# Moving the position transform of a hybrid encoder layer into the tiles of the projection's second half, and cutting the copies of the bias rows into 24

## The chip, the cores and the metric

The kernel runs on one core of one Trainium2 chip. The metric is the device time of one execution in microseconds (us). A profiled execution gives a trace of every instruction on the engines: PE is TensorE's matmul, PEld its weight load, DVE is VectorE, ACT is ScalarE, POOL is GpSimd, SP is SyncE, whose queue ("SPq") issues all the data transfers of this kernel.

## The reference

One layer of an encoder over two sequences of 4096 and 2048 tokens ("a" and "b"), with a model width of 1024:

```python
h = rmsnorm(x, norm_g)
proj = h @ w_in
q, k, v, g_attn, u, g_four = jnp.split(proj, [768, 1536, 2304, 3072, 3328], axis=-1)
# attention: 12 heads, three dilated windows, merged by their denominators; gated by silu(g_attn)
uf = u.astype(jnp.float32).reshape(B, S, N_FOURIER_GROUPS, FOURIER_GROUP)
mixed = jnp.fft.fftn(uf, axes=(1, 3), norm="ortho").real
four = jnp.einsum('bsgc,gce->bsge', mixed.astype(x.dtype), w_four).reshape(B, S, D_FOURIER)
four = four * jax.nn.silu(g_four)
y = jnp.concatenate([attn, four], axis=-1) @ w_out
return x + y
```

The change concerns the transform over positions (axis 1 of `fftn`) and the table of attention biases.

## The kernel before

`build` runs six stages one after the other; each is a block of five engine programs, and the engines meet between blocks: `setup`, `project(core, 0)`, `project(core, 1)`, `fourier`, `attention`, `combine`.

**The projection's first half** goes through 48 tiles of 128 tokens. Per tile it loads x (`load_x`, two tiles ahead), normalizes, splits into a high and a low part (`p_h_hi`, `p_h_lo`), keeps both parts in scratch memory for the second half (`keep_h`), and multiplies by the columns of q, k and u: four products per tile in the order 3, 0, 1, 2, each of 8 x 3 matmuls (`product`, L474). Product 3 is u (256 columns); it is transformed over channels at once (`turn_u` L481, `channel_dft` L489) and stored as `scratch_ab`, 512 floats per token. Behind the last weight load and ahead of `load_x(2)`, SP issues three transfers (L368) which write each row of 384 biases 128 times into `scratch_line`: 12 heads x 128 copies x 1536 bytes, for three dilations.

On DVE, tile 0 is special: the copy that `channel_dft(0)` waits for (L743) stands behind `norm_x(2)` and `head_norm(0, c=2)`. On ACT `norm_x(2)` (L535) stands ahead of the squares of product 2.

**The second half** goes through the same 48 tiles with the columns of v, the gates: per tile `load_h(t + 2)` (two transfers, L340, waiting until the last product of tile t is done), then a wait for the tile's four results, then `store_v` (14 transfers, L389 and L394) and one store of the gate (L433). Tiles 2, 4, 6 and 8 also turn the bias rows (`turn_lines`: a load of 1.5 MB, a copy on POOL, a store of 1.5 MB). The tile loop of PE, ACT and DVE is a hardware loop over two tiles (`Fori`); SP's is written out.

**The stage `fourier`** transforms `scratch_ab` over positions in two levels. A level-1 piece is a slice of columns of all rows, multiplied by one table (128x128 for a, 64x64 for b), and goes to `scratch_g_a` or `scratch_g_b`; a level-2 piece reads that, multiplies each 256 columns by another 128x64 table, and goes to `scratch_four`, which only `combine` reads. Level 2 needs all of level 1 of its sequence. There are 14 pieces of 4096 columns: 4 + 4 of level 1, 4 + 2 of level 2. Six buffers for input, four for output, eight PSUM banks; DVE and ACT copy the banks out in turn (L912). Piece 0 is already loaded during the second half of the projection.

**`attention`** starts with loads (L1104 first) that don't read what `fourier` wrote.

Of the kernel before, what the change touches and what calls it, by code (L numbers as in the profile page):

```python
# [25 lines left out]
P = 128  # L26
D = 1024
HD = 64
NH = 12
# [17 lines left out]
LINE = 384  # L47
VW = HD + 1
# [5 lines left out]
PIECE = 8 * BANK  # L54
# [53 lines left out]
def build(nc, io):  # L108
    core = Core(nc, io)
    with core.keep:  # L110
# [16 lines left out]
        with ExitStack() as spectrum:  # L127
            core.four_in = core.sb(spectrum, "four_in0", [P, PIECE])
            core.four_first = {n: core.sb(spectrum, "four_first_" + n, [2 * seq // N2, 2 * seq // N2])
                               for n, seq in zip("ab", SEQS)}  # L130
            core.four_in_loaded, core.four_table_in = core.sem("four_loaded0"), core.sem("four_table_in")
            project(core, 1)
            fourier(core)
# [81 lines left out]

def project(core, half):
# [22 lines left out]
    else:  # L239
        h_in, ones_done = [S("h_in0"), S("h_in1")], S("ones_done")  # L240
        expo_done, v_tail_done = S("expo_done"), S("v_tail_done")
        line_in, lines_turned, lines_kept = S("line_in"), S("lines_turned"), S("lines_kept")
    stored = [S("stored0"), S("stored1")]
# [21 lines left out]
    def tiles(engine, step):  # L265

        step(0, 0)
        step(1, 1)
        with engine.Fori(1, TILES // 2 - 1) as it:
            step(it * 2, 0)  # L270
            step(it * 2 + 1, 1)
        step(TILES - 2, 0)
        step(TILES - 1, 1)

    with ExitStack() as st:
# [22 lines left out]
        else:  # L298
            rows = [sb(f"v{i}", [P, VROW]) for i in range(2)]
            gate = [sb(f"gate{i}", [P, D]) for i in range(2)]  # L300
            expo, denom = sb("expo", [P, BANK]), sb("denom", [P, BANK])
        ps = [core.ps(st, name(f"ps{c}")) for c in range(4)]
        if half == 0:
            ps_t = [core.ps(st, name(f"ps_t{c}")) for c in range(banks_t)]
            ps_qk = [core.ps(st, name(f"ps_qk{c}")) for c in range(2)]
        block = st.enter_context(nc.Block())
# [17 lines left out]
        def _(sp):  # L324
# [37 lines left out]
            if half == 1:  # L362
                for n in "ab":
                    sp.dma_start(core.four_first[n][:], io["c_first_" + n]).then_inc(core.four_table_in, 16)
# [47 lines left out]
            def step(t, s):  # L412
# [8 lines left out]
                if half == 0:  # L421
# [5 lines left out]
                    if s == 1:  # L427
                        store_qk(t + 1, 0)
                else:
# [3 lines left out]
                    sp.dma_start(dram["gate"][lane_rows(t), :], gate[s][:]).then_inc(stored[s], 16)  # L433

            for t in range(TILES):
                step(t, t % 2)
            if half == 0:
                store_qk(TILES, 1)
                store_qk(TILES, 2)
                for c in range(3):  # L440
                    sp.wait_ge(qk_stored[c], 16 * (TILES // 2))
            else:
                sp.wait_ge(lines_kept, 32)
            if half == 0:
# [4 lines left out]
            if half == 0:  # L449
                sp.wait_ge(lines_out, 16 * len(DILS))  # L450

        @block.tensor
        def _(pe):
# [11 lines left out]
            def product(t, s, c):  # L465
# [10 lines left out]
                ins.then_inc(mm_done[c], 1)  # L476

# [26 lines left out]
            def step(t, s):  # L504
# [27 lines left out]
        def _(act):  # L532
# [49 lines left out]

            def gate_exp(t, c):
# [7 lines left out]
            def step(t, s):  # L591
# [12 lines left out]
                else:  # L604
                    for c in order:
# [3 lines left out]
                        if c > 0:  # L609
                            gate_exp(t, c)  # L610

# [162 lines left out]

class Piece:


    def __init__(self, name, seq, base, level, i):
        self.name, self.seq, self.base, self.level, self.i = name, seq, base, level, i
        self.n1 = seq // N2
        self.rows = 2 * self.n1 if level == 1 else 2 * N2
        self.out_rows = 2 * self.n1 if level == 1 else N2


def fourier_pieces():

    both, each = list(zip("ab", SEQS, BASES)), PIECE // DF  # L790
    return ([Piece(*seq, 1, i) for seq in both for i in range(N2 // each)]
            + [Piece(*seq, 2, i) for seq in both for i in range(seq[1] // N2 // each)])


def load_piece(core, sp, at, to, loaded):

    each = slice(at.i * PIECE // DF, (at.i + 1) * PIECE // DF)
    if at.level == 1:
        src = core.dram["ab"][at.base:at.base + at.seq, :].rearrange("(a b) (s c) -> s a b c", b=N2, s=2)
    else:  # L800
        src = core.dram["g_" + at.name].rearrange("(s k) (n c) -> s n k c", s=2, c=DF)
    half = at.rows // 2
    for part in range(2):
        sp.dma_start(to[part * half:(part + 1) * half, :].rearrange("p (n c) -> p n c", c=DF),
                     src[part, :, each, :]).then_inc(loaded, 16)


def fourier(core):

    nc, io, dram = core.nc, core.io, core.dram
    S = lambda n: core.sem("four_" + n)
    BANKS, IN, OUT = 8, 6, 4
    k1s = PIECE // DF
    pieces = fourier_pieces()
    fine_in = S("fine_in")  # L820
    loaded = [core.four_in_loaded] + [S(f"loaded{i}") for i in range(1, IN)]
    mm_done, out_done = S("mm_done"), [S("dve_out"), S("act_out")]
    stored = [S(f"stored{i}") for i in range(OUT)]
    with ExitStack() as st:
        sb = lambda n, shape: core.sb(st, "four_" + n, shape)
        first = core.four_first
        second = {n: sb("second_" + n, [2 * N2, seq]) for n, seq in zip("ab", SEQS)}
        source = [core.four_in] + [sb(f"in{i}", [P, PIECE]) for i in range(1, IN)]
        result = [sb(f"out{i}", [P, PIECE]) for i in range(OUT)]
        ps = [core.ps(st, f"four_ps{i}") for i in range(BANKS)]  # L830
        block = st.enter_context(nc.Block())

        @block.sync
        def _(sp):
            def load(m):
                if m >= IN:
                    sp.wait_ge(mm_done, BANKS * (m - IN + 1))
                load_piece(core, sp, pieces[m], source[m % IN], loaded[m % IN])

            def store(m):  # L840
                at = pieces[m]
                for evac in out_done:
                    sp.wait_ge(evac, BANKS // 2 * (m + 1))
                have = result[m % OUT][0:at.out_rows, :]
                if at.level == 1:
                    to = dram["g_" + at.name][:, at.i * PIECE:(at.i + 1) * PIECE]
                else:
                    to = dram["four"][at.base:at.base + at.seq, :].rearrange("(b a) c -> b a c", a=at.n1)
                    to = to[:, at.i * k1s:(at.i + 1) * k1s, :]
                    have = have.rearrange("p (k c) -> p k c", c=DF)  # L850
                sp.dma_start(to, have).then_inc(stored[m % OUT], 16)

            def spectrum_stored(name):

                for m, at in enumerate(pieces):
                    if at.level == 1 and at.name == name:
                        sp.wait_ge(stored[m % OUT], 16 * (m // OUT + 1))

            for m in range(1, IN):
                load(m)  # L860
                if m == 4:
                    for n in "ab":
                        sp.dma_start(second[n][:], io["c_second_" + n]).then_inc(fine_in, 16)
            ready = IN
            for m, at in enumerate(pieces):
                store(m)

                while ready < len(pieces) and ready - IN <= m:
                    new = pieces[ready]
                    if new.level == 2:  # L870
                        last_g = max(i for i, x in enumerate(pieces) if x.level == 1 and x.name == new.name)
                        if m < last_g + (1 if new.name == "a" else 0):
                            break
                        if new.i == 0:
                            spectrum_stored(new.name)
                    load(ready)
                    ready += 1
            for i in range(OUT):
                sp.wait_ge(stored[i], 16 * len(range(i, len(pieces), OUT)))

        @block.tensor
        def _(pe):
            pe.wait_ge(core.four_table_in, 32)
            for m, at in enumerate(pieces):
                have = source[m % IN][0:at.rows, :]
                pe.wait_ge(loaded[m % IN], 32 * (m // IN + 1))
                if at.level == 2:
                    pe.wait_ge(fine_in, 32)
                for j in range(BANKS):
# [754 lines left out]
```

## Time and profile before

| | us |
|---|---|
| median of 3 runs | 4076.96 (4073.61 to 4079.73) |
| the profiled execution, its own time | 4074.14 |
| its span in the trace | 4072.4 |
| PE busy in it | 3766.3 (92%) |
| DVE, ACT, POOL busy | 2554.1, 1680.9, 400.9 |

The span is the time from the first to the last record; 1.7 us lie around it. The 40 slices on the page are 102 us each, digits are tenths. In the rows of busy time by stretch the columns are: the stretch and its length, then busy time and (in brackets) instructions of PE, PEld, DVE, ACT and POOL, the clock granted to PE (1.00 is 2.4 GHz, 0.50 is 1.2 GHz), the mean busy share of the DMA engines, and GB/s. A matmul's recorded end is modelled, so the pace of matmuls is better read from the distance of their starts than from their durations.

### The profile page before, as it was taken

To read this page: it belongs to the slowest core of one execution; us is meant where nothing else is said; L and a number is where in the kernel's file an instruction comes from. 1 tells how busy PE (TensorE), PEld (TensorE's weight loads), DVE (VectorE), ACT (ScalarE), POOL (GpSimd) and SP (SyncE) were. 2 spreads that over 40 slices of the span, in tenths; PEclk is the share of its full clock that TensorE was granted. 3 is DMA by queue.
4 is the path that set the end of the run, shared out by engine and by line. 5 is a ranking of instruction groups with operands and counts; after the bars stand their busy time and mean duration, and the time that the engine had idled before them with its cause. 6 is when DMAs were issued, how large, how long until landed. Compare 5 with 4: busy or idle time off the path is not lost. (4 is left out here: it accounts for less than half of the span.)

```text
span 4072.4 us, 100342 instructions
## 1 busy us (share of the span) xinstructions
PE 3766.3 (92%) x38254; PEld 3227.5 (79%) x38254; DVE 2554.1 (63%) x7710; ACT 1680.9 (41%) x4443; POOL 400.9 (10%) x674
## 2 busy tenths in 40 slices
PE   3599999999997999999997859999999999799999
PEld 2488888888886888888884349999989898688887
DVE  3356666666655454445443248888888888777775
ACT  2233333333322111111111148898888888333332
POOL 0000000000000000000000024333342432000000
PEclk7799999999998999999998689999999999899999
DMA  6534444444437554444446996777768675666664
GB/s 131 126 134 154 163 145 140 139 170 142 152 124 234 184 156 141 146 145 144 142 145 168 269 281 169 211 188 188 205 167 214 155 204 137 228 243 244 239 249 175
DMA packets 604151, 721.86 MB, mean 177 GB/s; under 512 B 37215, under 2 KB 473567, under 8 KB 602112
## 3 DMA queue, kind: packets, MB, share of 16 engines
q1 hardware_dynamic: 603840, 717.55, 59.1%
q8 instruction: 215, 3.52, 0.4%
q14 instruction: 96, 0.79, 0.1%
HBM read 383.67 MB, written 337.94 MB: 177 GB/s over the span
## 5 line engine op out<-in xcount | busy, mean ns | idle before, releaser
L474 PE MATMUL p_ps<-p_w_hi,p_h_hi 128*128 128x512 f32 (+1 forms) x3072 | 1144.6, 373 | 22.2 <-DVE p_w_lo L756 20.7
L474 PE MATMUL p_ps<-p_w_lo,p_h_hi 128*128 128x512 f32 (+1 forms) x3072 | 1123.3, 366 | 0.0
L474 PE MATMUL p_ps<-p_w_hi,p_h_lo 128*128 128x512 f32 (+1 forms) x3072 | 1122.6, 365 | 0.0
L1289 ACT ACTIVATE att_p<-att_p,att_o 128x256 f32<-128x256 f32 (+2 forms) x1728 | 682.8, 467 | 125.2 <-DVE att_o L1347 124.2
L474 PEld LDWEIGHTS p_ps<-p_w_hi,p_h_hi 128*128 128x128 f32 x3072 | 582.0, 189 | 116.8 <-issue 18.4
L474 PEld LDWEIGHTS p_ps<-p_w_hi,p_h_lo 128*128 128x128 f32 x3072 | 581.2, 189 | 97.2
L474 PEld LDWEIGHTS p_ps<-p_w_lo,p_h_hi 128*128 128x128 f32 x3072 | 582.2, 190 | 92.1
L1347 DVE CUSTOM_DVE_ANT_0 att_p<-att_ps_s,att_bias 128x256 f32<-128x256 f32 (+2 forms) x1728 | 560.6, 381 | 59.4 <-PE att_ps_s L1227 54.3
L1260 PE MATMUL att_ps_o<-att_v,att_p_low 128*64 128x65 f32 x6528 | 439.7, 225 | 7.7 <-issue 7.4
L1260 PE MATMUL att_ps_o<-att_v,att_p_high 128*64 128x65 f32 x6528 | 439.5, 225 | 7.4 <-issue 7.2
L1260 PEld LDWEIGHTS att_ps_o<-att_v,att_p_low 128*64 128x64 f32 x6528 | 406.3, 140 | 24.6 <-issue 9.6
L1260 PEld LDWEIGHTS att_ps_o<-att_v,att_p_high 128*64 128x64 f32 x6528 | 406.3, 140 | 8.8 <-issue 8.7
L711 DVE RECIPROCAL p_denom<-p_denom 128x256 f32<-128x256 f32 x144 | 329.2, 2286 | 4.9
L1358 DVE COPY att_p_high<-att_ps_high 128x512 f32<-128x512 f32 x384 | 265.0, 690 | 100.8 <-PE att_ps_high L1242 98.7
L709 DVE TENSOR_SCALAR p_denom<-p_expo 128x256 f32<-128x256 f32 x144 | 48.7, 338 | 444.3 <-ACT p_expo L588 444.3
L1491 PE MATMUL out_ps_y<-out_w_hi,out_m_hi 128*128 128x512 f32 x768 | 308.6, 402 | 2.3 <-DVE out_m_lo L1591 2.3
L1491 PE MATMUL out_ps_y<-out_w_hi,out_m_lo 128*128 128x512 f32 x768 | 304.3, 396 | 0.0
L1491 PE MATMUL out_ps_y<-out_w_lo,out_m_hi 128*128 128x512 f32 x768 | 304.1, 396 | 0.0
L1242 PE MATMUL att_ps_low<-ident,att_p 64*128 64x64 f32 x3264 | 289.5, 227 | 11.7 <-issue 8.8
L1242 PE MATMUL att_ps_high<-ident,att_p 64*128 64x64 f32 x3264 | 291.2, 228 | 4.1 <-issue 4.1
L677 DVE TENSOR_REDUCE p_sumsq<-p_squares 128x8 f32<-128x512 f32 x144 | 98.8, 686 | 291.1 <-ACT p_squares L553 291.1
L553 ACT ACTIVATE p_squares<-p_ps 128x512 f32<-128x512 f32 x144 | 86.1, 598 | 451.3 <-PE p_ps L474 451.3
(111 smaller groups left out, 5216.4 us busy)
## 6 DMA issues: line engine op xcount, KB each, us to landing
scratch_qk<-p_staging SPq DMA_DIRECT2D x72, 1024.0 KB, 5.8
out_o<-scratch_o SPq DMA_DIRECT2D x144, 396.0 KB, 5.4
att_qk_a<-scratch_qk SPq DMA_DIRECT2D x192, 256.0 KB, 4.5
scratch_o<-att_o SPq DMA_DIRECT2D x168, 264.0 KB, 3.3
p_x<-x SPq DMA_DIRECT2D x48, 512.0 KB, 4.4
scratch_h_t<-p_h_hi SPq DMA_DIRECT2D x48, 512.0 KB, 5.4
scratch_h_t<-p_h_lo SPq DMA_DIRECT2D x48, 512.0 KB, 6.2
p_h_hi<-scratch_h_t SPq DMA_DIRECT2D x48, 512.0 KB, 3.9
```

What stands on the lines that cost most here:

```text
L474: ins = pe.matmul(ps[c][:, 0:width[c]], a[s][:, k, :], b[:, k, cols], start=(k == 0 and n == 0), stop=(k == KC - 1 and n == 2))
L553: act.activation(squares[:], ps[c][:], ACT.Square).then_inc(sq_done, 1)
L677: dve.tensor_reduce(sumsq[:], squares[:].rearrange("p (h w) -> p h w", w=HD), AX.X, ALU.add).then_inc(chain, 1)
L709: dve.tensor_scalar(denom[:, w], expo[:, w], 1.0, None, ALU.add).then_inc(chain, 1)
L711: dve.reciprocal(denom[:, w], denom[:, w]).then_inc(chain, 1)
L1242: ins = pe.transpose(to[:, ((2 * i + e) * 2 + j) * HD:((2 * i + e) * 2 + j + 1) * HD], p[q % RING][rows, i, e, at:at + P], core.ident[rows ...
L1260: ins = pe.matmul(ps_o[q % 2][lo:lo + HD, to:to + VW], have[q % RING][:, i, e, j, :], v[n % BUFS][:, chunk, e * VW:(e + 1) * VW], start=(j ...
L1289: ins = act.activation(at, at, ACT.Exp, bias=o[n % BUFS][:, (2 * q + i) % STRETCH, PW + e:PW + e + 1], scale=-1.0)
L1347: dve.tensor_tensor_reduce(p[q % RING][:, i, e, 0:u.w], ps_s[q % 2][e][:, 2 * P * i:2 * P * i + u.w], bias[:, u.d, e, u.lo:u.lo + u.w], -1 ...
L1358: ins = dve.tensor_copy(p_high[q % RING][:], have)
L1491: ins = pe.matmul(ps_y[2 * s + c][:], a[s][:, k, :], b[:, k, c * BANK:(c + 1) * BANK], start=(k == 0 and n == 0), stop=(k == KC - 1 and n ...
```

## The change

The stage `fourier` and its buffers are removed. In `project(core, 1)` every engine's loop is written out instead of running in hardware, and tile t (from 2 to 29) also carries piece m = t - 2 of 28 pieces of 2048 columns (8 + 8 of level 1, 8 + 4 of level 2):

- PE: behind products 3 and 0 of the tile, `transform(m)`: 4 fp32 matmuls of 512 columns (level 1) or 8 of 256 columns (level 2), into four more PSUM banks.
- ACT: behind the work on product 1, `copy_piece(m)`, four copies of 512 columns.
- SP: behind `store_v` and the gate's store of tile t, `store_piece(t - 2)` and `load_piece(t)`, two transfers, with a third for a slice of the level-2 table. Pieces 0 and 1 are loaded behind the weights. There are two input and two output buffers.

In the first half the three broadcast transfers at the start become 24, each of 16 of the 128 copies of one dilation, issued at the end of SP's work for tiles 8 to 31.

```diff
-PIECE = 8 * BANK
+PIECE = 4 * BANK
+PIECE_FIRST = 2
+LINE_PARTS, LINE_FIRST = 8, 8
 ...
-            project(core, 1)
-            fourier(core)
+        project(core, 1)
 ...
     def tiles(engine, step):
+        if half == 1:
+            for t in range(TILES):
+                step(t, t % 2)
+            return
 ...
-                load_piece(core, sp, fourier_pieces()[0], core.four_in, core.four_in_loaded)
-            else:
-                for i in range(len(DILS)):
-                    sp.dma_start(dram["line"][i].rearrange("h (a j) -> h a j", a=P), core.line[:, i * LINE:(i + 1) * LINE]
-                                 .rearrange("h (a j) -> h a j", a=1).broadcast_to([NH, P, LINE])).then_inc(lines_out, 16)
+            def load_piece(m):
+                at = pieces[m]
+                if m >= 2:
+                    sp.wait_ge(piece_done, m - 1)
+                if at.level == 2:
+                    last_first = max(i for i, x in enumerate(pieces) if x.level == 1 and x.name == at.name)
+                    for i in range(2):
+                        sp.wait_ge(piece_out[i], 16 * len(range(i, last_first + 1, 2)))
+                    n = PIECE // DF * N2
+                    sp.dma_start(dft_fine[m % 2][:], io["c_second_" + at.name][:, at.i * n:(at.i + 1) * n]).then_inc(fine_in[m % 2], 16)
+                for to, have in at.loads(dram, dft_in[m % 2]):
+                    sp.dma_start(to, have).then_inc(piece_in[m % 2], 16)
+            def store_piece(m):
+                sp.wait_ge(piece_copied, 4 * m + 4)
+                to, have = pieces[m].out_store(dram, dft_out[m % 2])
+                sp.dma_start(to, have).then_inc(piece_out[m % 2], 16)
+            def spread_line(k):
+                d, rows = k // LINE_PARTS, P // LINE_PARTS
+                at = k % LINE_PARTS * rows
+                sp.dma_start(dram["line"][d].rearrange("h (a j) -> h a j", a=P)[:, at:at + rows, :],
+                             core.line[:, d * LINE:(d + 1) * LINE]
+                             .rearrange("h (a j) -> h a j", a=1).broadcast_to([NH, rows, LINE])).then_inc(lines_out, 16)
 ...
+                    if LINE_FIRST <= t < LINE_FIRST + LINE_PARTS * len(DILS):
+                        spread_line(t - LINE_FIRST)
 ...
                     sp.dma_start(dram["gate"][lane_rows(t), :], gate[s][:]).then_inc(stored[s], 16)
+                    m = t - PIECE_FIRST
+                    if 0 <= m < len(pieces):
+                        store_piece(m)
+                        if m + 2 < len(pieces):
+                            load_piece(m + 2)
 ...
+            def transform(m):
+                at = pieces[m]
+                have = dft_in[m % 2][0:at.rows, :]
+                if m == 0:
+                    pe.wait_ge(first_in, 32)
+                pe.wait_ge(piece_in[m % 2], 32 * (m // 2 + 1))
+                if at.level == 2:
+                    pe.wait_ge(fine_in[m % 2], 16 * n_fine(m))
+                for j in range(4):
+                    if m:
+                        pe.wait_ge(piece_copied, 4 * m - 3 + j)
+                    if at.level == 1:
+                        ins = pe.matmul(ps_dft[j][0:at.out_rows, :], dft_first[at.name][:], have[:, j * BANK:(j + 1) * BANK],
+                                        start=True, stop=True)
 ...
+                ins.then_inc(piece_done, 1)
 ...
                     product(t, s, c)
+                    if half == 1 and n == 1 and 0 <= t - PIECE_FIRST < len(pieces):
+                        transform(t - PIECE_FIRST)
 ...
+            def copy_piece(m):
+                n = pieces[m].out_rows
+                act.wait_ge(piece_done, m + 1)
+                if m >= 2:
+                    act.wait_ge(piece_out[m % 2], 16 * (m // 2))
+                for j in range(4):
+                    act.activation(dft_out[m % 2][0:n, j * BANK:(j + 1) * BANK], ps_dft[j][0:n, :],
+                                   ACT.Copy).then_inc(piece_copied, 1)
```

## Rows read from the trace of the kernel before

**Rows 1.** Busy time by stretch: setup and start, stall, first half, second half, and on.

```profile
64.00:147.00 83.00, 0.00 (x0) 0.00 (x0) 4.20 (x16) 2.04 (x5) 0.00 (x0) 0.51 0.63 84
147.00:1229.00 1082.00, 1078.61 (x5734) 913.13 (x5734) 666.31 (x2142) 353.12 (x975) 0.00 (x0) 1.00 0.43 147
1300.00:2125.00 825.00, 825.00 (x4123) 703.64 (x4123) 403.83 (x386) 96.08 (x215) 11.25 (x2) 1.00 0.51 152
```

**Rows 2.** Timeline of PE around tile 0's end (start, length, in brackets idle before).

```profile
63.34 0.38 PE L481 MATMUL p_ps<-ident,p_u 128*128 128x128 f32 x2
147.22 2.08 PE L489 MATMUL p_ps<-chan_w,p_ut 128*128 128x256 f32 x4 [83.50 <-DVE p_ut L743]
```

**Rows 3.** Timelines of SP's queue and of ACT in the same stretch.

```profile
40.30 43.37 SPq L368 DMA_DIRECT2D scratch_line<-line  x3
83.71 31.26 SPq L328 DMA_DIRECT2D p_x<-x  x1
...
47.15 1.06 ACT L615 ACTIVATE p_w_hi<-p_staging 128x1024 fp32r<-128x1024 f32 x1 [1.16 <-DMA p_staging<-w_in]
...
56.97 0.60 ACT L568 ACTIVATE p_staging<-p_ps_qk 128x512 fp32r<-128x512 f32 x1 [0.17 <-PE p_ps_qk L500]
140.70 1.06 ACT L535 ACTIVATE p_squares_x<-p_x 128x1024 f32<-128x1024 f32 x1 [83.13 <-DMA p_x<-x]
...
142.18 0.58 ACT L553 ACTIVATE p_squares<-p_ps 128x512 f32<-128x512 f32 x1
```

**Rows 4.** Timeline of SP's queue from the last tile of the second half into attention.

```profile
2194.63 26.18 SPq L804 DMA_DIRECT2D four_in<-scratch_ab  x8
...
2370.91 7.80 SPq L1104 DMA_DIRECT2D qk_b<-scratch_qk  x16
```

**Rows 5.** Timeline of PE in the stage fourier.

```profile
2227.77 7.13 PE L894 MATMUL four_ps<-four_in,four_first_a 128*128 128x512 f32 x16 [2.60 <-DMA four_in<-scratch_ab]
2234.83 7.08 PE L894 MATMUL four_ps<-four_in,four_first_b 64*64 64x512 f32 x16
2251.95 41.19 PE L894 MATMUL four_ps<-four_in,four_first_b 64*64 64x512 f32 x48 [10.04 <-DVE four_out L912]
...
2310.07 7.09 PE L899 MATMUL four_ps<-four_in,four_second_a 128*64 128x256 f32 x32 [0.49 <-DVE four_out L912]
```

**Rows 6.** Timeline of SP's queue over one tile of the second half.

```profile
2117.70 0.33 SPq L340 DMA_DIRECT2D p_h_hi<-scratch_h_t  x1
...
2131.89 0.75 SPq L433 DMA_DIRECT2D scratch_gate<-p_gate  x1
2136.92 0.33 SPq L340 DMA_DIRECT2D p_h_hi<-scratch_h_t  x1
```

**Rows 7.** Busy time, columns as in the first group: plain tiles, tile with lines, fourier.

```profile
1302.00:1321.20 19.20, 19.20 (x98) 16.37 (x97) 9.42 (x9) 2.24 (x5) 4.19 (x1) 1.00 0.74 222
...
1500.00:1596.00 96.00, 96.00 (x481) 81.90 (x480) 46.96 (x45) 11.21 (x25) 0.00 (x0) 1.00 0.48 144
...
2194.60:2370.90 176.30, 128.66 (x320) 54.59 (x320) 37.19 (x56) 31.79 (x56) 0.00 (x0) 0.78 1.03 256
```

**Rows 8.** The piece buffers: matmul durations (ns, min/median/max), and issue to landing.

```profile
L899 PE MATMUL four_ps<-four_in,four_second_a x128: 379/379/687, 2293.1 to 2330.3; 128*64 128x256 f32 x128
...
L894 PE MATMUL four_ps<-four_in,four_first_a x64: 592/592/1190, 2194.8 to 2234.3; 128*128 128x512 f32 x64
...
DMA to landing us min/median/max: 7.2/16.2/21.7
```

**Rows 9.** Timelines of SP's queue and of ACT in a tile of the first half.

```profile
606.51 0.43 SPq L328 DMA_DIRECT2D p_x<-x  x1
...
626.31 1.05 ACT L535 ACTIVATE p_squares_x<-p_x 128x1024 f32<-128x1024 f32 x1
```

**Rows 10.** Busy time and clock in four stretches: broadcast alone, and 64x64 matmuls.

```profile
83.70:115.00 31.30, 0.00 (x0) 0.00 (x0) 0.00 (x0) 0.00 (x0) 0.00 (x0) 0.50 0.67 76
...
2235.00:2240.00 5.00, 5.00 (x12) 1.48 (x12) 0.00 (x0) 0.53 (x1) 0.00 (x0) 1.00 1.02 323
...
2270.00:2280.00 10.00, 10.00 (x13) 2.62 (x12) 2.21 (x4) 1.73 (x4) 0.00 (x0) 0.50 0.86 275
```

More of the change, by code:

```diff
@@ L125, in build @@
             project(core, 0)
[L127 to L131, printed above, removed]
-            project(core, 1)
-            fourier(core)
+        project(core, 1)
         core.qk_b = core.sb(core.keep, "qk_b", [P, 4, SEQS[1]], F32R)
@@ L211, in _, with __init__, loads, out_store @@
                 dve.tensor_copy(core.chan_w[:, gp, :], ps_chan[gp][:, 0:2 * P])
+class Piece:
+    def __init__(self, name, seq, base, level, i):
+        self.name, self.seq, self.base, self.level, self.i = name, seq, base, level, i
+        self.n1 = seq // N2
+        self.rows = 2 * self.n1 if level == 1 else 2 * N2
+        self.out_rows = 2 * self.n1 if level == 1 else N2
+    def loads(self, dram, to):
+        each = slice(self.i * PIECE // DF, (self.i + 1) * PIECE // DF)
+        if self.level == 1:
+            src = dram["ab"][self.base:self.base + self.seq, :].rearrange("(a b) (s c) -> s a b c", b=N2, s=2)
+        else:
+            src = dram["g_" + self.name].rearrange("(s k) (n c) -> s n k c", s=2, c=DF)
+        n = self.rows // 2
+        return [(to[s * n:(s + 1) * n, :].rearrange("p (n c) -> p n c", c=DF), src[s, :, each, :]) for s in range(2)]
+    def out_store(self, dram, have):
+        have = have[0:self.out_rows, :]
+        if self.level == 1:
+            return dram["g_" + self.name][:, self.i * PIECE:(self.i + 1) * PIECE], have
+        k1s = PIECE // DF
+        to = dram["four"][self.base:self.base + self.seq, :].rearrange("(b a) c -> b a c", a=self.n1)
+        return to[:, self.i * k1s:(self.i + 1) * k1s, :], have.rearrange("p (k c) -> p k c", c=DF)
+def fourier_pieces():
+    both, each = list(zip("ab", SEQS, BASES)), PIECE // DF
+    return ([Piece(*seq, 1, i) for seq in both for i in range(N2 // each)]
+            + [Piece(*seq, 2, i) for seq in both for i in range(seq[1] // N2 // each)])
 def project(core, half):
@@ L305, in project @@
             ps_qk = [core.ps(st, name(f"ps_qk{c}")) for c in range(2)]
+        else:
+            ps_dft = [core.ps(st, name(f"ps_dft{c}")) for c in range(4)]
         block = st.enter_context(nc.Block())
@@ L443, in _ @@
                 sp.wait_ge(lines_kept, 32)
+                for i in range(2):
+                    sp.wait_ge(piece_out[i], 16 * len(range(i, len(pieces), 2)))
             if half == 0:
@@ L476, in product @@
                 ins.then_inc(mm_done[c], 1)
+            def transform(m):
[12 more added lines that the diff above has]
+                                        start=True, stop=True)
+                    else:
+                        for i in range(2 * j, 2 * j + 2):
+                            ins = pe.matmul(ps_dft[j][0:N2, i % 2 * DF:(i % 2 + 1) * DF],
+                                            dft_fine[m % 2][:, i * N2:(i + 1) * N2], have[:, i * DF:(i + 1) * DF],
+                                            start=True, stop=True)
+                ins.then_inc(piece_done, 1)
             def turn_u(t):
@@ L610, in step @@
                             gate_exp(t, c)
+                        if c == 1 and 0 <= t - PIECE_FIRST < len(pieces):
+                            copy_piece(t - PIECE_FIRST)
             def split_w(n):
@@ L773, in _ @@
                 qk_lo(TILES - 1, 1, 2)
[L778 to L792, printed above, removed]
@@ L795, in load_piece @@
[L795 to L805, printed above, removed]
@@ L808, in fourier @@
[L808 to L889, printed above, removed]
-                    if m >= 1:
-                        pe.wait_ge(out_done[j % 2], BANKS // 2 * (m - 1) + j // 2 + 1)
-                    if at.level == 1:
-                        ins = pe.matmul(ps[j][0:at.out_rows, :], first[at.name][:], have[:, j * BANK:(j + 1) * BANK],
-                                        start=True, stop=True)
-                    else:
-                        for i in range(2 * j, 2 * j + 2):
-                            k1 = at.i * k1s + i
-                            ins = pe.matmul(ps[j][0:N2, i % 2 * DF:(i % 2 + 1) * DF],
-                                            second[at.name][:, k1 * N2:(k1 + 1) * N2],
-                                            have[:, i * DF:(i + 1) * DF], start=True, stop=True)
-                    ins.then_inc(mm_done, 1)
-        def copies(engine, parity):
-            for m, at in enumerate(pieces):
-                if m >= OUT:
-                    engine.wait_ge(stored[m % OUT], 16 * (m // OUT))
-                for j in range(parity, BANKS, 2):
-                    engine.wait_ge(mm_done, BANKS * m + j + 1)
-                    to, have = result[m % OUT][0:at.out_rows, j * BANK:(j + 1) * BANK], ps[j][0:at.out_rows, :]
-                    ins = engine.activation(to, have, ACT.Copy) if parity else engine.tensor_copy(to, have)
-                    ins.then_inc(out_done[parity], 1)
-        @block.vector
-        def _(dve):
-            copies(dve, 0)
-        @block.scalar
-        def _(act):
-            copies(act, 1)
```

14 lines of the change are left out of this document (12 added, 2 removed).

## The prediction

> **What bounds the kernel now.** I read the busy time by stretch first, to see the stages apart. In the second half of the projection PE is busy for all of 825 us of 825 and its granted clock is 1.00 [rows 1]: there every matmul added lengthens the kernel by its own pace, and nothing else bounds it. The first half is nearly the same (1078.6 of 1082), but in front of it lie 83 us in which PE does nothing [rows 1]. Then I went to the timelines for the two places that the change removes. First, what ends the stall: PE waits 83.50 us for DVE's copy L743 [rows 2]; that copy stands behind `norm_x(2)` in program order, ACT's half of it waits 83.13 us for the transfer x(2), and x(2) is issued at 83.71 because the three broadcasts hold SP's queue from 40.30 for 43.37 us, and then itself takes 31.26 us to issue [rows 3]. So the broadcast bounds this place. Second, the stage `fourier`: SP's first issue in it is at 2194.63, its first issue in attention at 2370.91 [rows 4]. PE is busy 128.66 of those 176.3 us and the 16 DMA engines have a busy share of 1.03 [rows 7]: this stage is bound by transfers, and the projection before it has transfer time to spare (0.48).
>
> **1. The stage goes: -176.3 us.** What attention waits for at its start doesn't depend on `fourier`. Before, the meeting of the engines at the end of the second half released SP at 2194.63; afterwards it releases attention's first load there, one meeting fewer, and no tile after 29 carries a piece, so its stores are long landed by tile 47. 2370.9 - 2194.6 = 176.3 [rows 4].
>
> **2. The transform on PE comes back in the tiles: +97.2 us.** PE is full there, so its pace counts. Each fp32 matmul has two records. Level 1, a: 16 records in 7.13 us, the last 0.59 long, so (7.13 - 0.59)/15 = 0.436 us apart; a piece has 8, 3.49 us. Level 1, b: (7.08 - 0.59)/15 = 0.433, 3.46 us. Level 2: 32 records in 7.09, the last 0.38 long, 0.2165 apart, 16 a piece, 3.46 us [rows 5, 8]. 8 x 3.49 + 8 x 3.46 + 12 x 3.46 = 97.1; with rounding 97.2. Their weight loads are shorter than the pace of the matmuls and run beside them. Below this it can't be (a full PE hides nothing); above, the neighbouring fp32r products may pass more slowly when ACT reads PSUM more. One bound for a slower passage: the first half, where ACT is busier, takes no PE idle either; I allow 0.3 us a piece, an estimate, 8 us, and take 1 of them.
>
> **3. ACT, DVE, SP in the tiles: 0.** ACT is busy 11.21 of 96 us, 2.2 a tile [rows 7]; four copies of 0.6 us make it 4.7 of 22.7. It waits for nothing new at that place: `transform` stands ahead of product 1 on PE, and the output buffer was stored two tiles earlier. If that cover were gone, product 2's gate would be late by 2.4 us, against a product order in which its bank is needed 17 us later. SP: from the first L340 of a tile to that of the next 19.22 us pass, of which the issues fill the stretch up to 2132.6, 14.9 us [rows 6]. The new issues add three, four in level 2, of some 0.5 us when the rings have room: about 17 of 22.7. Behind them on SP stand `turn_lines` and `load_h(t + 3)`; the latter is needed a whole tile later. Tile length becomes 19.22 + 3.47 = 22.7.
>
> **4. Do the transfers keep up?** A plain tile has 0.48 x 19.2 = 9.2 us of DMA time. All of `fourier` is 1.03 x 176.3 = 182 us, over 28 pieces 6.5 on average [rows 7]. The heaviest (level 1 of a, level 2) are about 7.5, so 16.7 of 22.7 us, a share of 0.74; with the line load, whose tile stands at 0.74 instead of 0.48 (+5 us), 21.7, a share of 0.96 [rows 7]. It fits, without much room. The time that matters: load(t) is issued some 16 us after the end of product 2 of tile t (14.9 plus the piece's store); its transform stands in tile t + 2 behind products 3 and 0, 2.9 + 5.4 us in. That is 22.7 + 8.3 - 16 = 15 us for issue to landing. Ahead of it in the queue are the rest of the gate and the piece's store, together with itself about 9 us of transfer, and 2 for latency: 11 us. I take no stall, and keep both ends: the landings in the saturated stage have median 16.2 and longest 21.7 [rows 8].
>
> **5. The stall at tile 0 goes, but for its own chain: -78.8 us.** x(2) is issued at 40.3 instead, behind the weights, whose last part was there at 47.15 [rows 3]; it lands at about 49. ACT reaches `norm_x(2)` after 56.97 + 0.6, so it waits for nothing. Then the squares of product 2, which in the trace stand at 142.18, follow the product's end at 63.4, and PE continues as long after them as it did: 147.22 - 142.18 = 5.04 [rows 2, 3], at 68.4. Saved: 147.22 - 68.4 = 78.8. PE ran at half clock when it came back (2.08 us for L489 [rows 2]); a shorter pause may spare 1.5 us of that, which I leave in the range. If x(2) were still late, tile 1 would wait for it.
>
> **6. The 24 small copies in tiles 8 to 31: 0.** The broadcast alone moves 76 GB/s at a share of 0.67 [rows 10]; 7.08 MB over 24 is 295 KB, 3.9 us each. The load of x behind it is issued at 606.51 and first used at 626.31 [rows 9], 19.8 us. With 3.9 ahead of it, and 7.2 for its own landing (the shortest of the piece loads, transfers of the same size or twice it [rows 8]), it is 8.7 us early; the share goes from 0.43 by 2.6 us of DMA time in some 23 us to 0.54 [rows 1]. Gone the cover: 24 x 3.9 = 93 us. That the share stays at two thirds with nothing else running says that the broadcast doesn't reach all DMA engines. The Trainium skill, in "DMA: Bandwidth & Descriptors", section "Why a DMA increments its semaphore by 16 and not by 1", says that a transfer goes over the largest number up to 16 that divides its slowest dimension; with 12 heads there that would be 12. The trace's 0.67 agrees roughly (0.75 would be 12 of 16), and the small copies keep those 12 heads outermost, so they are as slow per byte.
>
> **7. Loops written out: 0.** The looped tiles show no idle PE time at all [rows 1], so nothing is gained at the loop's edge. The Trainium skill ("Runtime: NRT & Kernel Launch", "Instruction fetch mechanics") says sequential code is prefetched and a taken branch may stall; this trace has no such stall, so by that rule too nothing is won or lost.
>
> **Sum:** 4074.1 - 176.3 - 78.8 + 97.2 + 1 = 3917.2 on the profiled execution's own time, which lies 2.8 below the median; rounded 3917.
>
> **Rivals.**
> *A: the piece loads land late.* With the median of the saturated stage, 16.2 instead of 15, each of the 28 tiles waits 1.2 us, 34 us: 3951. For it: two buffers only, a share near 1 in tiles with lines. Against: the queue is not six transfers deep here.
> *B, the other side: every piece lands as late as the latest.* The same place, the wait of `transform` for its input; at 21.7 us the tile waits 6.7, 28 x 6.7 = 188: 4105, slower. It decides from a landing of 21.0 us, where 28 x 6.0 eats the 157 won and 0.2% more. Against it: 16.7 us of transfers in a tile of 22.7 can't hold such a queue for long.
> *C: small matmuls and the clock.* 64x64 matmuls run for 41 us without pause at a granted clock of 0.50, although PE is busy 10 of 10 us; when they followed 128x128 ones they kept 1.00 for at least 5 us [rows 5, 10]. If the 8 pieces of b's first level pull the clock down, each takes 3.5 us more and the products behind it run some 4 us at half pace, 2 us more: 8 x 5.5 = 44, 3961. Against: 3.5 us of them at a time, between full products. The Trainium skill ("TensorE: Matmul & The Clock Gate", "What's actually happening") says activity releases the clock; that busy time alone doesn't do it here is what the row shows.
> *D: the first half gives some back*, by copies that delay x or by a remaining stall: a quarter of the 93 us, 3940.
> *E: the broadcast isn't what holds x(2)*, so the stall stays: 3996. The issue times speak against it.
>
> **Chances:** forecast 0.66, A 0.12, B 0.03, C 0.07, D 0.09, E 0.03. Below the forecast lie 1.5 us of clock and little else; the likeliest case itself reaches from 3908 to 3930. The range takes in A and D: 3904 to 3953. Measurement can tell 0.2%, about 8 us, from no change: faster 0.965, same 0.005, slower 0.03.
>
> **What would show it.** No L8xx stage: attention's first L1104 directly behind the last L433 by about 5 us. Second half: its length grows by 97 us, tiles 2 to 29 take 22.7 us, the rest 19.2, PE without idle time and at clock 1.00; DMA share near 0.75. An idle PE ahead of the transform, released by a piece's load, would be A or B; a clock below 1 in tiles 10 to 17, C. PE's pause after 63.7 is about 5 us and tile 1 begins near 71. ACT's L535 and PE in tiles 8 to 31 wait for nothing. Wrong would make it: landings above 15 us, or products slower beside the new copies.

## The result and the profile after

| | us |
|---|---|
| before, 4 runs beside it | 4078.35 median (4073.61 to 4080.11) |
| after, 4 runs | 3900.22 median (3898.42 to 3901.64) |
| ratio | 0.9565, 95% interval 0.9548 to 0.9581 |
| the profiled execution after, its own time | 3901.64 |
| its span | 3899.9 |

The kernel is faster by 4.35%, and by 17 us more than forecast (3917): the time lies 4 us below the low end of the range, 3904. Of the forecast's terms the two large savings came out as they were worked out, the cost of the transform on PE was 6.5 us too small, and a stage that the prediction hadn't in its sum became 22 us shorter.

To see where, cut both traces at the same issues of SP: the first `load_h` of the second half, the first load of `fourier`, of attention and of `combine`.

| stretch, us | before | after | difference | forecast |
|---|---|---|---|---|
| to the second half's first `load_h` | 1238.16 | 1159.42 | -78.7 | -78.8 |
| from there through the second half | 956.47 | 1061.17 | +104.7 | +98.2 |
| `fourier` | 176.28 | none | -176.3 | -176.3 |
| attention | 1089.98 | 1068.07 | -21.9 | 0 |
| `combine` | 611.5 | 611.2 | -0.3 | 0 |

The sum, -172.5, takes the own time 4074.1 to 3901.6. Attention's length is the distance from its first load (2370.91 before [rows 4], 2220.59 after) to the first load of `combine`, before and after:

```profile
3460.89 1.30 SPq L1445 DMA_DIRECT2D out_o<-scratch_o  x3
```

```profile
3288.66 1.31 SPq L1414 DMA_DIRECT2D out_o<-scratch_o  x3
```

The stall first. The timeline of PE of the kernel after, around tile 0's end, with the lines that answer to [rows 2]:

```profile
64.60 0.38 PE L584 MATMUL p_ps<-ident,p_u 128*128 128x128 f32 x2
68.72 2.07 PE L592 MATMUL p_ps<-chan_w,p_ut 128*128 128x256 f32 x4 [3.74 <-DVE p_ut L860]
...
71.67 0.54 PE L555 MATMUL p_ps<-p_w_hi,p_h_hi 128*128 128x256 f32 x1
```

The timeline of SP's queue in the same stretch, where x(2) stands behind the weights [against rows 3]:

```profile
40.74 0.47 SPq L373 DMA_DIRECT2D p_x<-x  x1
```

x(2) takes 0.47 us to issue instead of 31.26, the pause is 3.74 us instead of 83.50, and the channel transform begins at 68.72, where 68.4 was forecast. It still runs at half the pace (2.07 us for four matmuls).

Busy time by stretch of the kernel after: the start, a tile of a's level 1 with lines, b's level 1, and level 2.

```profile
64.00:147.00 83.00, 79.24 (x426) 67.11 (x425) 49.22 (x158) 27.10 (x76) 0.00 (x0) 0.98 0.41 137
...
1232.00:1255.00 23.00, 23.00 (x107) 18.17 (x106) 11.43 (x10) 4.50 (x11) 5.64 (x1) 1.00 0.68 216
...
1440.00:1600.00 160.00, 160.00 (x731) 121.09 (x730) 65.89 (x63) 29.14 (x63) 0.00 (x0) 1.00 0.60 172
1600.00:1800.00 200.00, 200.00 (x977) 159.70 (x976) 82.25 (x78) 34.90 (x75) 0.00 (x0) 1.00 0.74 199
```

PE is full in every one of the stretches of the second half, and the granted clock is 1.00, in 1440 to 1600 too, where the 64x64 matmuls of b run. The transfers keep up, at a share of 0.60 to 0.74 in these stretches and of 0.80 from 1255 to 1440, which is the rest of a's level 1, more tiles with lines among them, and the first tile or two of b's. The view of the input buffers of the pieces, `p_dft_in` (durations in ns, min/median/max; last the time from issue to landing):

```profile
L423 SPq DMA_DIRECT2D p_dft_in<-scratch_g_a x16: 636/1350/2241, 1573.2 to 1736.5; - x16
...
who waited for it (us, times):
...
DMA to landing us min/median/max: 5.4/8.0/12.9
```

Nobody waited for a piece, and the latest landed after 12.9 us, where 15 were free.

The tiles of the second half, read as the distance of their first L385: 22.71 us in tiles with a piece of a's level 1, 23.06 with one of b's, 23.04 with one of level 2, 19.22 in those without. One tile of SP's timeline in level 2, with the piece's transfers:

```profile
1671.16 0.33 SPq L385 DMA_DIRECT2D p_h_hi<-scratch_h_t  x1
...
1686.17 0.88 SPq L429 DMA_DIRECT2D scratch_four<-p_dft_out  x1
1687.18 0.92 SPq L421 DMA_DIRECT2D p_dft_fine<-c_second_a  x1
1688.14 2.83 SPq L423 DMA_DIRECT2D p_dft_in<-scratch_g_a  x2
1694.20 0.33 SPq L385 DMA_DIRECT2D p_h_hi<-scratch_h_t  x1
```

SP is done at 1690.97, 19.8 us into a tile of 23.04; forecast were 17. Over all tiles that load a piece, but the first, this round of SP takes 18.2 to 20.9 us.

The way out of the stage, on SP's queue [against rows 4]:

```profile
2215.97 0.74 SPq L507 DMA_DIRECT2D scratch_gate<-p_gate  x1
2220.59 5.59 SPq L1073 DMA_DIRECT2D qk_b<-scratch_qk  x11
```

3.9 us lie between the end of the last store's issue and attention's first load. So far the forecast holds. What is left is attention, whose code the change doesn't touch. The waits of PE there, before (in total, times, longest):

```profile
PE att_ps_s L1227 <- POOL att_q L1184: 48.2, 7, 28.5
PE att_ps_o L1260 <- issue: 14.6, 22, 2.0
PE att_ps_low L1242 <- issue: 8.8, 19, 0.7
PE att_ps_s L1227 <- issue: 6.6, 10, 2.5
PE att_ps_high L1242 <- issue: 4.1, 7, 1.5
```

and after, where all line numbers of attention are 31 lower:

```profile
PE att_ps_s L1196 <- POOL att_q L1153: 56.8, 7, 35.3
PE att_ps_o L1229 <- issue: 17.3, 25, 1.7
PE att_ps_low L1211 <- issue: 3.1, 7, 0.9
...
PE att_ps_s L1196 <- issue: 1.3, 2, 0.9
PE att_ps_high L1211 <- issue: 0.3, 1, 0.3
```

"Issue" is idle time for which the trace has no semaphore: 34.1 us in 58 pieces before, 22.0 in 35 after. In the transposes (L1242) and scores (L1227) it falls from 19.5 to 4.7 us, in the weighing matmuls (L1260) it rises from 14.6 to 17.3. Idle time isn't all of the 22 us: between PE's first and last matmul of attention, 1070.2 us before and 1048.1 after, idle time is 11.2 us less and recorded busy time 10.9 us less for the same 24,768 matmul records. Adding up the distances from each start to the next takes in both: the scores fall from 372 to 364 us, the transposes from 250 to 237, the weighing matmuls from 448 to 446. So 21 of the 22 us lie in the transposes and the scores.

### The profile page after: what moved, and what is told of

Read it like the earlier page. It is cut to its first block and busy times, and to the rows that moved or that the text cites. A ratio compares the mean times of both kernels' runs of the same rounds, so it can differ in the third digit from the quotient of the medians.

```text
span 3899.9 us, 99819 instructions
## 1 busy us (share of the span) xinstructions
PE 3731.8 (96%) x38254; PEld 3210.4 (82%) x38254; DVE 2516.6 (65%) x7654; ACT 1702.4 (44%) x4499; POOL 400.3 (10%) x674
```

## The experiments

Their ratios are to runs of the kernel before on the same chip.

**1. The copies of the bias rows alone.** The kernel before with only the spreading:

```diff
+LINE_PARTS, LINE_FIRST = 8, 8
 ...
-                for i in range(len(DILS)):
-                    sp.dma_start(dram["line"][i] ...
+                    if LINE_FIRST <= t < LINE_FIRST + LINE_PARTS * len(DILS):
+                        spread_line(t - LINE_FIRST)
```

> The kernel before with one part of the change: the 24 small copies of the bias rows in tiles 8 to 31 in place of the three at the start. Theory (the broadcast holds x(2), and nothing else changes): the first product of tile 1 starts at 71.7 us instead of 150.2, every later stage keeps its length, the whole is 78.5 us faster, about 3998. Rival (some of the surprising 22 us in attention come from this part): more than 85 us faster, with a shorter attention stage.

Measured: 3998.17 us, ratio 0.9805 (0.9788 to 0.9821), so 80 us less, as expected. The first part is shorter by 79.3 us (1158.83), `fourier` as long as before (176.7), attention 1093.6, so 3.7 us longer. The 78.8 us belong to this edit, and the shortening of attention doesn't.

**2. The written-out loops alone.** The kernel before with:

```diff
+        if half == 1:
+            for t in range(TILES):
+                step(t, t % 2)
+            return
```

> The kernel before with only the loops of the second half written out. Theory U (attention's program now starts at another place in the stream of instructions, or is fetched otherwise, and that alone made it 22 us shorter): attention, from its first transfer issue to combine's first, takes about 1068 us instead of 1090, the whole is 18 to 24 us faster, the second half of the projection keeps its length. Rival V (attention is shorter because the stage of the transform isn't ahead of it): attention stays at 1090 us and the whole is within 5 us of before.

Measured: 4052.99 us, ratio 0.9944 (0.9931 to 0.9957): some 23 us faster. The second half keeps its length, 956.63 us against 956.47; attention has 1068.15 instead of 1089.98. Theory U came out: writing out the loops of one stage speeds up a later one. This is all of the unforecast 22 us.

**3. Full-width tables.** The kernel after, with every matmul of the transform on an array of 128x128; b's level 1 takes a's table and both levels fill rows that nothing reads, so the values of the transform are other ones:

```diff
-ps_dft[j][0:at.out_rows, :], dft_first[at.name][:], have[...]
+ps_dft[j][:], dft_first["a"][:], dft_in[m % 2][...]
 ...
+w = min(i, 6)
-ps_dft[j][0:N2, ...], dft_fine[m % 2][:, i * N2:(i + 1) * N2]
+ps_dft[j][:, ...], dft_fine[m % 2][:, w * N2:(w + 2) * N2]
```

> The changed kernel with every transform matmul on the full 128x128 array: the pieces of b's first level use a's table and all 128 rows, the second level multiplies by two neighbouring 64-column tables at once into 128 rows; the values of b's first level and of unused rows are other ones, the numbers of matmuls, their columns and all transfers are the same. Theory (the 0.35 us that tiles 10 to 29 take above 22.71 are the change between a full and a partly used array): all 28 tiles with a piece take 22.71 us, the whole is 20 x 0.34 = 7 us faster. Rival (they come from the transfers' or the table's form): tiles 10 to 29 stay at 23.05, no change.

Measured: 3895.28 us, ratio 0.955 (0.9534 to 0.9565). All tiles of level 1 now take 22.71 us, those of level 2 22.73; attention is unchanged (1068.0). The second half is 5.9 us shorter, where 7 were expected for the whole; the rival, no change, is out. The timelines of PE show where: first the kernel after, b's first piece,

```profile
1402.44 0.39 PE L555 MATMUL p_ps<-p_w_hi,p_h_lo 128*128 128x512 f32 x1
1402.76 3.64 PE L572 MATMUL p_ps_dft<-p_dft_in,p_dft_first_b 64*64 64x512 f32 x8
1406.33 0.50 PE L555 MATMUL p_ps<-p_w_hi,p_h_hi 128*128 128x512 f32 x1
1406.67 0.40 PE L555 MATMUL p_ps<-p_w_lo,p_h_hi 128*128 128x512 f32 x1
```

and the same piece with the full-width table:

```profile
1403.75 0.40 PE L555 MATMUL p_ps<-p_w_hi,p_h_lo 128*128 128x512 f32 x1
1403.98 3.60 PE L572 MATMUL p_ps_dft<-p_dft_in,p_dft_first_a 128*128 128x512 f32 x8
1407.01 0.79 PE L555 MATMUL p_ps<-p_w_hi,p_h_hi 128*128 128x512 f32 x1
1407.64 0.39 PE L555 MATMUL p_ps<-p_w_lo,p_h_hi 128*128 128x512 f32 x1
```

The step into the piece is 0.32 us against 0.23, the way from its first matmul to the second one behind it 3.91 against 3.66: 0.34 us in all. The matmuls of a narrow array are no slower among themselves (8 records in 3.64 us, the last 0.59 long, so 0.436 us apart, as with the full one); going in and out costs.

**4 to 6. Where the program of attention begins in its blocks of instructions.** PE's instructions are themselves brought by transfers: the trace has 198 in attention of 16,384 bytes each on the instruction queue, one for about every 125 matmuls. Counting PE's records (weight loads, matmuls and semaphore waits) in order of time and calling every 256th a block change, with the first one placed where most gaps fit, 53 of the 58 "issue" gaps before lie within 8 records of a change, and 29 of 35 after; by chance it would be one in 15. By that fit attention begins some 84 to 94 places into a block before (from 84 on it is at least 52 of 58), and 2 to 17 after: the written-out loops only shifted where attention's instructions lie. At which matmuls the changes then stand, and at how many of them PE shows a gap, is in the table below. Theory P says that this place alone makes the 22 us; its rival, that it is the history of the loop. One line in front of attention's code on PE sets the place, in blocks of 256 instructions: offset 0 in the kernel after (4) and in the kernel before (5, hardware loops and all), offset 84 in the kernel after (6).

```diff
+            pe.addr_align(256, offset=0)    # 84 in 6
```

> The changed kernel; PE's program for attention is moved by padding so that its first instruction opens a block of instructions. Nothing else changes, and PE skips the padding at a place where it waits. Theory U2 (where the borders of fetched blocks fall in PE's program sets how often PE runs dry in attention): the attention stage moves from 1068 us by some 5 to 25 us in either direction. Rival V2 (it is not PE's place in the stream): 1068 within 3 us.

> The kernel before, with loops and all, and only PE's program for attention moved by padding so that its first instruction opens a block of 256 fetched instructions. Theory P (place in the stream): in both runs with attention at 1090 and 1094 us the borders of the blocks lie some 40 matmuls away from where they lie in the four runs with 1068 to 1072, so attention falls from 1090 to about 1070 us and the whole to about 4057, as with written-out loops. Rival H (the loop itself, run before, leaves the fetching of instructions later): attention stays at 1090 to 1094 us, the whole at 4078.

> The changed kernel with PE's program for attention moved by padding so that its first instruction stands 84 places behind the opening of a block, where it stood in the kernel before. Theory P (place): attention rises from 1068 to about 1090 us, the whole to about 3921. Rival H (the loop): attention stays at 1068 to 1072 us, the whole at 3900.

| | us | ratio (95%) | attention | changes (with a gap) at weighing / transposes / scores | PE "issue" | transposes |
|---|---|---|---|---|---|---|
| before | 4078 | 1 | 1090.0 | 87 (23) / 56 (20) / 55 (9) | 34.1 | 250.2 |
| 5: before, place 0 | 4053.9 | 0.994 (0.9918 to 0.9963) | 1066.9 | 127 (21) / 39 (1) / 32 (2) | 17.8 | 237.2 |
| after | 3900.2 | 0.9565 (0.9548 to 0.9581) | 1068.1 | 123 (25) / 45 (2) / 30 (2) | 22.0 | 237.1 |
| 4: after, place 0 | 3899.5 | 0.9566 (0.9552 to 0.958) | 1071.8 | 127 (20) / 41 (1) / 30 (0) | 17.4 | 236.6 |
| 6: after, place 84 | 3931.2 | 0.9639 (0.9616 to 0.9663) | 1096.8 | 87 (23) / 59 (21) / 52 (7) | 40.0 | 259.6 |

The last column is the time of the transposes, from each start to the next, in us. The counts are for places 84 before and 8 after; they can be off by a few, since weight loads and matmuls overlap in time.

The kernel before gets 24 us without any part of the change, and the changed one loses 31 by one line. The history of the loop is out. In 5 theory P came out in size too; in 6 it had the direction, and the loss was half as large again as expected (31 us against 21). 4 moved the whole by less than 1 us, and attention by 3.8 in its profiled execution, where 5 to 25 were expected: the place of after lay near 0 anyway. That run also shows that the padding by itself costs nothing to speak of, since it has more of it (247 empty instructions) than 5 (169) and 6 (75).

It isn't the mere number of changes at transposes that counts: that number goes from 56 to 45 between before and after, while those with a gap go from 20 to 2. At place 84 a third of the changes at transposes show a gap, at place 0 hardly any; why, these runs don't say. At the weighing matmuls there are 20 to 25 gaps at either place. The waits of PE in attention of 5,

```profile
PE att_ps_o L1260 <- issue: 13.6, 21, 1.6
PE att_ps_low L1242 <- issue: 2.1, 6, 0.4
PE att_ps_s L1227 <- issue: 2.0, 2, 1.2
```

and of 6:

```profile
PE att_ps_o L1229 <- issue: 17.9, 23, 2.0
PE att_ps_low L1211 <- issue: 9.2, 14, 1.4
PE att_ps_high L1211 <- issue: 9.0, 13, 1.7
PE att_ps_s L1196 <- issue: 3.9, 7, 0.9
```

PE's "issue" time is 23 us more in 6 than in 4, and its transposes take 23 us more. DVE, which reads what they write, waits for them longer (84.9 us in 174 pieces in 4). Its waits for the transposes in attention, in 6 and in 5:

```profile
DVE att_p_high L1328 <- PE att_ps_high L1211: 106.0, 199, 2.4
```

```profile
DVE att_p_high L1359 <- PE att_ps_high L1242: 78.1, 169, 1.8
```

One gap as it looks in PE's timeline, of 6:

```profile
2634.85 0.22 PE L1211 MATMUL att_ps_low<-ident,att_p 64*128 64x64 f32 x1
2635.86 0.21 PE L1211 MATMUL att_ps_high<-ident,att_p 64*128 64x64 f32 x1 [0.78 <-issue]
```

Transposes otherwise start some 0.06 us apart; here one comes a microsecond late and no wait that the trace records held it. That a gap costs the stage less at weighing matmuls, because no engine waits at once for them, is a guess that was not tried by itself.

**7 to 9. How much room do SP and the transfers have?** Each piece is stored again, 4, 1 or 2 times more, into memory that nobody reads:

```diff
+EXTRA = 4                               # 1 in 8, 2 in 9
 ...
+                for x in range(EXTRA):
+                    sp.dma_start(dram["spare"][m, x, 0:rows, :], dft_out[m % 2][0:rows, :]).then_inc(piece_out[m % 2], 16)
```

> The changed kernel with each piece stored four more times, to unused scratch memory, ahead of the load of the piece that comes two tiles later; 10 us more transfer time in the 8 tiles of a's first level, 5 us in the other 20. It asks how much room the transfers had. Theory (room of 15 us from issue to landing, 8 used): the 20 tiles with 5 us more stay at 23.05 us, the 8 with 10 us more are 2 to 4 us longer, since 18 us of landing are 3 above the room and 26 us of transfers don't fit in 22.7; the whole some 25 us slower, 3925. Rival B (hardly any room): all 28 tiles become longer by 3 us or more, 3985 or above. Rival N (transfers never bind): within 5 us of 3900.

> As the run with four extra stores per piece, but with one. That run made tiles of every kind some 27 us long; its extra issues alone hold SP's queue for 8.5 us a tile, 2.1 each. Theory S (SP's own round of issues is the room: 18.5 us of 22.7 in the first level of a, 19.8 of 23.04 in the second level, so 4.2 and 3.2 us free): one store more fits, tiles stay within 0.1 us, the whole within 5 us of 3900. Rival T (landing behind a fuller queue is what cost the time): even one store more lengthens tiles, the heavy ones by 1 us or more, 3915 or above.

> The same with two extra stores per piece: 4.2 us more of issuing. Theory S: SP's round becomes 22.7 in the first level of a (just full) and 24.0 in the second level, so the 12 tiles of the second level get about 1 us longer each, the whole 3905 to 3920. Rival T: all tiles longer by 2 us or more, 3950 or above.

| extra stores | us | ratio (95%) | second half | PE waits for `p_dft_in` |
|---|---|---|---|---|
| 0 | 3900.2 | 0.9565 | 1061.2 | 0 |
| 1 (8) | 3901.93 | 0.958 (0.9564 to 0.9596) | 1062.2 | 0.8 |
| 2 (9) | 3925.86 | 0.964 (0.9624 to 0.9656) | 1089.5 | 21.5 |
| 4 (7) | 4030.76 | 0.9894 (0.9868 to 0.992) | 1190.2 | 83.2 |

SP's queue in a tile of level 2 of 9:

```profile
1617.75 0.33 SPq L386 DMA_DIRECT2D p_h_hi<-scratch_h_t  x1
...
1633.66 1.10 SPq L430 DMA_DIRECT2D scratch_four<-p_dft_out  x1
1634.80 3.76 SPq L433 DMA_DIRECT2D scratch_spare<-p_dft_out  x2
1638.68 2.23 SPq L422 DMA_DIRECT2D p_dft_fine<-c_second_a  x1
1640.95 2.78 SPq L424 DMA_DIRECT2D p_dft_in<-scratch_g_a  x2
1643.77 0.62 SPq L386 DMA_DIRECT2D p_h_hi<-scratch_h_t  x1
```

SP's round has grown from 19.8 to 26.0 us, and the next `load_h` follows it without a pause: in this tile, the longest of level 2, SP has no time left at its end. It isn't the only one: in 16 of the last 18 tiles that load a piece (22.7 to 26.0 us long) SP's round ends at most 0.1 us ahead of the next `load_h`. There SP's queue sets the length of the tile. An extra store costs SP 1.88 us to issue, the table's slice 2.23 instead of 0.92. The DMA engines are near their limit as well; 9's busy time by stretch over level 2:

```profile
1600.00:1800.00 200.00, 191.43 (x918) 151.14 (x917) 75.81 (x74) 33.89 (x73) 0.00 (x0) 0.99 0.93 235
```

A share of 0.93 instead of 0.74. Long issues and a high share come together, so these runs don't say whether the issues would be as long with idle DMA engines. Of the 28 us that the second half of 9 is longer, 13 lie in level 2, about 1 a tile, as expected, and 11 in two tiles of a's level 1 with lines (28.5 and 28.3 us), in which PE waits 4.4 and 3.6 us for its input; the expectation hadn't these, so the whole came out 6 us above its 3905 to 3920. Rival T, 3950 or above, is out.

One extra store costs next to nothing (theory S of 8): there is room for one more such transfer a tile and not for two. With four (7) the expectation, 3925, failed by 106 us. All tiles with a piece but the first take 24 to 34 us, most of them 26 to 28; the share is 0.97 from 1600 to 1800, and the granted clock falls to 0.91 to 0.95 from 1200 on. That is the time that rival B gave (3985 or above), but not for B's reason, since 8 and 9 show that there was room: four more issues of some 2 us each, which the expectation hadn't counted, don't fit into SP's round. Of the 129 us PE waits 83 for its input; how much of the rest is the lower clock wasn't separated. In 9 attention has 1059.8 us, 8 less than in after; the cause stays open.

## Why the prediction was right or wrong

**Step 1 (-176.3), right.** The stage goes whole, and attention begins 3.9 us behind the last store's issue (about 5 was forecast).

**Step 5 (-78.8), right.** Measured 78.7 in the trace of after, 79.3 in experiment 1. Rival E is out. The broadcast held x(2), and its issue time was the thing to read.

**Step 2 (+97.2 and 1 of allowance), right in mechanism, too small by 6.5 (104.7 measured).** The pace inside a piece is as worked out from [rows 5]; a's tiles became 19.22 + 3.49 = 22.71 us to the digit. But 20 of the 28 pieces use a narrow array, between products that use the full one, and each of these tiles is longer by 0.35 us (b's) or 0.33 (level 2): 8 x 0.35 + 12 x 0.33 = 6.8. Experiment 3 removes it. The 8 us bound of the prediction (0.3 us a piece, for slower passage of the products beside ACT) was of the right size with a wrong reason: a's eight tiles, with the same copies on ACT, show nothing of it. That size was luck. [Rows 5] come from a stage in which such matmuls run in long unbroken rows, so the price of going in and out once a tile couldn't be read there.

**Step 3 (0), right, but with less room than stated.** ACT and SP delay nothing. SP's round is 18.2 to 20.9 us instead of about 17, above all because issuing a piece's two loads takes 1.7 to 3.7 us, not 1. Experiment 9 shows that PE does wait when the round fills the tile.

**Step 4 (no stall), right.** Landings of at most 12.9 us against 15 (11 were worked out), a share of 0.74 in level 2 as worked out, and 0.68 to 0.80 where lines are turned instead of 0.96. Rivals A and B are out; experiments 8 and 9 show how far: with one extra store a tile PE waits 0.8 us for late pieces in all, with two 21.5.

**Rival C, out.** The clock stays at 1.00 through all of b's pieces.

**Step 6 (0), right.** In the trace no one waits for x in tiles 8 to 31, and from tile 1 on the first half is as long as before: 1159.42 - 71.67 = 1087.75 us against 1087.99. Rival D is out.

**Step 7 ("Loops written out: 0"), wrong.** This is the step that took the time out of the range. It looked for the effect in the tiles of the written-out stage, and there it is in fact nothing (956.6 us, experiment 2). Its sentence that "this trace has no such stall" holds for the looped tiles of [rows 1] and wasn't looked into for attention. There it costs and saves: another number of instructions on PE in front of attention shifts attention's code against the blocks in which it is fetched, and with it the matmuls at which PE runs dry. That is worth -21.9 us here, some -23 in experiment 2, -24 in 5 and +31 in 6. The Trainium skill ("Runtime: NRT & Kernel Launch", "Instruction fetch mechanics") has the blocks of 256 instructions, and says that crossing a border is "mostly hidden". The size agrees with the trace's 16,384 bytes. "Mostly hidden" is true of the count, since 146 of 198 borders show no gap before and 169 after. It is not true of the sum: PE has 16 to 43 us of "issue" time in attention in the eleven kernels, most of it at such borders, and how much depends on the place. The trace of before had 34.1 us of "issue" there, unexplained, and the prediction didn't read it. Had it, the sign would still have been open, since where the code would fall couldn't be seen in that profile, but a range with some 25 us each way for it would have held the result.

By the sum: 4074.1 - 176.3 - 78.7 + 104.7 - 21.9 - 0.3 = 3901.6. Without the shift in attention the kernel would be at 3923.5, inside the likeliest case's 3908 to 3930. The two errors, -21.9 and +6.5, have opposite signs; it is luck that the time lies only 4 us outside the range and not 10.

**Left open:** what in a block change takes its microsecond, and why only some changes show it; why attention at the same place still differs between kernels (1066.3 in 7 to 1071.8 in 4, 1059.8 in 9; 1090.0 before against 1093.6 in 1). Each of these lengths comes from one profiled execution, and the whole times of one kernel's executions differ by as much: 3898.57 to 3906.15 in 4, whose profiled one, 3904.36, lies 5 us above its median. Of the 8 us of 9 that accounts for a part: its profiled execution, 3921.44, lies 4 us below its median.

## What to carry to other kernels

When a change alters the number of instructions on an engine, look at every later stage in which that engine issues many short instructions: its idle time put down to "issue" is what can move, here by 24 to 31 us of 4,000 for the whole, with no edit there. To judge such a change, pin the place of that stage's code in both kernels, or time the unrolling alone. A stage that another kernel's profile shows bound by transfers can be laid over one bound by PE for the pace of its matmuls alone, if transfers and the issue time of the queue both leave room in each tile; take issue times from a loaded stretch.

## What the runs showed of the hardware

- PE's instructions come in blocks of 16,384 bytes, and at 21 to 52 of the 198 block changes in attention PE shows a gap, mostly of 0.2 to 1.4 us (up to 2.5), at the others none. Moving the code by 84 places is worth 24 us (5) to 31 us (6) of 4,000.
- Going from a 128x128 array to a narrower one and back costs 0.31 to 0.35 us here (23.06 and 23.04 us a tile against 22.71 and 22.73 in 3); among themselves the narrow ones keep the pace.
- What it costs SP to issue one load or store of 0.5 MB depends on what stands ahead of it in the queue. In level 2 of after it is 0.33 us for `load_h`, the first of its round, and 0.88 to 1.4 for a piece's store and loads at the round's end; an extra store in 9 costs 1.88.
